# Start addresses on chip: normed activations on a 64-byte multiple, the arena 32 bytes above one

## The reference

```
h = rms_norm(x);  proj = h @ w_in                 # 1024 x 7168
m = rms_norm(mem);  mk, mv = split(m @ w_mem_kv)  # 1024 x 1024
merged = sum_b sigmoid(gate_b) * (attention_b(proj, mk, mv) @ w_branch_b)   # three kinds of attention
x = x + merged @ w_out
x = x + moe(rms_norm(x))     # 32 experts, top 4: (up + 1) * gate * sigmoid(1.702 gate), then w_down
out = rms_norm(x)
```

## Time and profile before

| | |
|---|---|
| median of 3 executions | 1217.89 us (1217.21 to 1218.4) |
| the profiled execution | 1218.3 us, its span 1216.5 us |
| granted TensorE clock, mean | 0.984 |
| TensorE matmul busy | 1166.8 us |
| moved by DMA | 455.15 MB, mean 374 GB/s |

### The profile page before, as it was taken

One profiled execution on the slowest core, in us unless ns is written; L12 is line 12 of the kernel. 1 busy time (PEld: TensorE's weight loads), 2 busy tenths in 40 slices (PEclk: granted clock), 3 DMA queues, 4 the chain that ended last, 5 costly groups with the idle time before them and its releaser, 6 DMA issues.

```text
span 1216.5 us, 14185 instructions
## 1 busy us (share of the span) xinstructions
PE 1166.8 (96%) x6145; PEld 595.8 (49%) x6145; DVE 246.4 (20%) x511; ACT 269.7 (22%) x579; POOL 206.4 (17%) x89
## 2 busy tenths in 40 slices
PE   8999999999999999999999999998999999999996
PEld 7989877898433333333343333333333333333332
DVE  3145132233411121111111211111111111111112
ACT  6457577445210111001010100100000000010002
POOL 5864766785000000000000000000000000000000
PEclk9999999999999999999999999999999999999999
DMA  8775644677999999999999999999999999999994
GB/s 278 262 244 198 212 155 154 226 278 256 424 430 431 430 434 434 415 435 432 431 432 432 430 434 433 433 432 433 433 430 431 431 430 432 430 432 431 431 431 207
DMA packets 62136, 455.15 MB, mean 374 GB/s; under 512 B 5129, under 2 KB 33705, under 8 KB 43512
## 3 DMA queue, kind: packets, MB, share of 16 engines
q1 hardware_dynamic: 62072, 454.22, 90.3%
HBM read 453.13 MB, written 1.07 MB: 373 GB/s over the span
## 4 chain that ended last, share of the span: by engine, by line
PE 65%; DMA 30%; ACT 2%; DVE 1%; POOL 1%; issue 1%; DVEq 0%; SPq 0%; ACTq 0%; POOLq 0%
PE ps L591 63%; DMA arena<-in_expert_w_gate_up 27%; DMA arena<-in_expert_w_down 3%; PE ps L904 1%; PE ps L646 1%; PE ps L898 1%; POOL w_lowc L580 0%; DMA arena<-in_mem 0%; POOL w_lowa L580 0%; ACT arena L1106 0%; ACT arena L1096 0%; ACT L1120 0%; ACT w_high L1076 0%; DVE x_normed L1562 0%; PE ps L642 0%
## 5 line engine op out<-in xcount | busy, mean ns | idle before, releaser
L591 PE MATMUL ps<-arena,gathered_T 128*64 128x512 f32 x2034 | 472.8, 613 | 29.2 <-DMA arena<-in_expert_w_gate_up 29.2
L591 PE MATMUL ps<-arena 128*64 128x512 f32 (+6 forms) x1490 | 316.4, 562 | 3.4 <-issue 2.1
L591 PEld LDWEIGHTS ps<-arena,gathered_T 128*64 128x64 f32 x2034 | 144.9, 140 | 296.5 <-issue 269.2
L591 PEld LDWEIGHTS ps<-arena 128*64 128x64 f32 (+3 forms) x1490 | 113.3, 149 | 196.2 <-issue 193.6
L1229 ACT COPY arena<-ps 128x256 f32<-128x256 f32 x32 | 11.9, 372 | 350.5 <-PE ps L898 350.5
L1506 DVE TENSOR_SCALAR arena<-arena 128x128 f32<-128x128 f32 x64 | 19.3, 344 | 307.2 <-PE ps L898 307.2
L1512 DVE TENSOR_SCALAR arena<-ps 128x512 f32<-128x512 f32 x32 | 22.1, 692 | 275.6 <-PE ps L591 275.6
L1220 ACT ACTIVATE gathered_T<-ps,g_cols 128x128 f32<-128x128 f32 x128 | 36.6, 368 | 173.4 <-PE ps L591 173.4
L591 PEld LDWEIGHTS ps<-arena,x_normed 128*128 128x128 f32 x512 | 59.5, 191 | 24.8 <-issue 24.3
L591 PE MATMUL ps<-arena,x_normed 128*128 128x128 f32 x512 | 65.4, 281 | 0.2 <-DVE arena L1463 0.2
L1239 ACT COPY arena<-ps 128x512 f32<-128x512 f32 x31 | 18.2, 586 | 172.2 <-PE ps L591 172.2
(11 more groups left out here) (229 smaller groups left out, 897.5 us busy)
## 6 DMA issues: line engine op xcount, KB each, us to landing
arena<-in_expert_w_gate_up SPq DMA_DIRECT2D x53, 4096.0 KB, 37.9
arena<-in_expert_w_down SPq DMA_DIRECT2D x61, 2048.0 KB, 38.2
arena<-in_expert_w_gate_up SPq DMA_DIRECT2D x19, 2048.0 KB, 10.8
arena<-in_w_in SPq DMA_DIRECT2D x29, 1024.0 KB, 5.2
arena<-in_expert_w_down SPq DMA_DIRECT2D x6, 1024.0 KB, 38.6
arena<-in_expert_w_gate_up SPq DMA_DIRECT2D x4, 1024.0 KB, 7.1
arena<-in_w_out SPq DMA_DIRECT2D x4, 1024.0 KB, 5.8
arena<-in_w_mem_kv SPq DMA_DIRECT2D x3, 1024.0 KB, 11.5
```

The source lines that it names most:

```text
L591: return nc.tensor.matmul(out, lhsT, rhs, start=start, stop=stop, **kw)
```

## The change

`eps` is allocated behind `h_T_parts`, no longer ahead of `x_tokens`. So `x_tokens` starts at 3328, `x_normed` at 11520, `h_T_parts` (with all that lies over it) at 19712: multiples of 64. What follows `eps` stands where it stood. The arena's start is rounded up to 64 and then raised by 32: it starts at 38944, 32 above a multiple of 64, and everything in it moves by 32. No instruction, DMA, wait or size changes.

```
-        eps = sb("eps", [P, 1])
         x = sb("x_tokens", [P, T, D])
         xn = sb("x_normed", [P, T, D])
         hHL = sb("h_T_parts", [P, 2, KC, S], F32R)
         h_at = nc.sbuf_base - 2 * KC * S * 4
+        assert h_at % 64 == 0
+        eps = sb("eps", [P, 1])
...
-        base = -(-nc.sbuf_base // 64) * 64
+        base = -(-nc.sbuf_base // 64) * 64 + 32
         MOE0 = RING * CHUNK
         arena = nc.alloc_sbuf_tensor_at("arena", [P, ARENA], F32, offset=base)
```

## The result

The changed kernel is slower: 1223.78 us median (1222.56 to 1225.81, 6 runs) against 1217.55 us (1215.71 to 1218.4, 6 runs) of the kernel before beside it, a ratio of 1.0054 [1.0043, 1.0065]. That is outside the range. All lines of the code stand one number higher in the changed kernel.

A forecast was written before the change was run, and what follows sets the result against it. PE bounds the front, transfers the expert stage from 307 us. Front matmul terms +0.9 - 0.5 - 1.6 + 0 gave -1.2 us, passed whole to the end: 1216.7 us against 1217.89, range 1213.4 to 1219.6.

The forecast's parts named there:

- Transfers into the arena: Expert weights landing 32 bytes higher: no loss taken; other end 1.4% of 881 us, 12 us.
- the fourth rival: Expert stage: transfers pay for the new start, visible from 3.6 us, at 1.4% about 1229 us; chance 0.05.
- Group 1: Front, twelve chunks with activations moving, 576 matmuls of 256 columns: 118.3 ns each, +0.9 us.
- group 2: Front, seven single chunks, 336 matmuls with activations stationary: 116.7 ns each, -0.5 us.
- group 4: Front, operand pairs within the arena (memory, branches, output): both operands move alike, 0 us.
- Group 3: Front, ten wide chunks, 240 matmuls of 512 columns, activations stationary: 226.7 ns each instead of 233.3, -1.6 us.
- only the difference counts: Front matmuls: only the two operand addresses' difference matters, so a swap does nothing, 1217.9 us; chance 0.17.
- the matmuls of the experts: Expert stage, float32 matmuls on PE: no loss, and any would be hidden under the transfers; nothing taken.
- ACT's casts: ACT's 82 casts: 1047 ns at remainder 0, 1046 at 32; nothing taken, bounds 0.1 us.
- falling GB/s: Full stretches of the expert stage should stay at 431 GB/s; a fall would make the prediction wrong.
- the price of a stationary operand: Rival for front matmuls: stationary operand 32 above a multiple costs 6.7 ns anywhere, +3.1 us, 1221.0 us; chance 0.07.

The follow-up runs named there:

- small loads and 32: Arena 32 bytes higher, against the small loads kernel with the arena at 38912: 1241.18 us, ratio 1.0201.
- relation kept: Kernel before with normed parts 32 below a multiple of 256, arena on one (39168), so arena minus normed parts as in the changed kernel: 1218.23 us, ratio 1.0005.
- small loads: Kernel before with weights of experts 4 to 30 (without 6 and part of 8) loaded chunk by chunk in 8 KB packets: 1225.41 us, ratio 1.0062.

## Why the prediction was wrong

**The step that failed** is "*Transfers into the arena.* ... I take nothing". It measured 4.1 us in the stream of expert weights, the fourth rival come true at a price between its 3.6 us of visibility and its 12: I gave it 0.05 and left it out of the range. Two things went wrong in that step. The one is the remainder: I had sorted every row by the remainder by 64, by which the arena at 38912 and one at 39040 are alike, while the runs tell the transfers apart by 256. The other is the witness. x's load to a start 32 above a multiple went at 444 GB/s, and I called that too rough for 0.2%. It was worse than rough: in the trace of before x's own packets of 8 KB take 309 ns at that very start, no price at all, and in the kernel with only the arena moved the same load to the same address takes 314 (medians). In all four kernels with x there and the arena off the boundary (32, 64, 128, small loads and 32) its median packet takes 313 or 314 ns, in the four with x there and the arena on it (before, 256, relation kept, small loads) 309. A single load off a boundary among others on it was no witness for a stream off it.

The Trainium skill had spoken against the change: DMA: Bandwidth & Descriptors, section "How a descriptor splits into AXI transactions", names the 256-byte boundary and a price per descriptor. It tells of bytes that are fetched, while what moved here is where the rows are written. The runs agree on both, the boundary (0 and 256 free, 32, 64 and 128 paid) and the price per row and not per byte. Its size does not agree: by that rule 32 bytes off costs one beat of 32 bytes, an estimate of 1.2 ns at the 16384 bytes in 611 ns of a row, and 128 bytes off four beats, 4.8 ns. Measured are 4.1 ns and, for 128, 2.9. I set that rule aside on the strength of a row that could not decide.

**Pairs of the front.** Group 1 held (+1.5 x 576 = +0.9 us), group 2 held (-0.5), group 4 held at nothing (memory pairs 119.8 and 119.6 ns, branches 228.1 in both). Between the first wide memory run and the bias load behind PE's last front chunk lie 297.41 - 26.14 = 271.27 us and before 297.68 - 26.83 = 270.85: +0.4, their sum. That this load was issued 0.3 us earlier, and not later, comes from a start 0.7 us earlier, which differs from execution to execution.

**Group 3** was mis-sized: -1.6 us forecast, 0 measured. I let the stationary operand's place decide. The table says that the difference of the two addresses does: before and with everything 256 higher, the same three durations; the changed kernel, the arena 64 higher and the kept relation, with three different pairs of places, again one set. Each difference tried but 0 (32, 96 and 224) leaves the wide products near 233; 0 gives 228. So the rival "only the difference counts" was right on what counts and wrong on what follows: the difference changes its sign, from 32 below to 32 above, and the two groups of 256 columns trade durations.

**The rest** held: the DMA share stays full, the matmuls of the experts and ACT's casts don't change, and PE in the expert stage stays covered by the transfers. What I said would make the prediction wrong, falling GB/s, is what did. Two small sums were off, without consequence: by its own words the range ends at 1217.9 + 1.9 = 1219.8 us, not 1219.6, and the price of a stationary operand decides from 5.3 ns on, not 5.4.

**What stays open.** The kernels with the arena off a multiple lose some 6 us by the medians, the packets from 330 us on account for 4.1. Of the profiles, the five off a multiple issue the bias load at 299.0 us on average (297.4 to 300.8), the five on one at 297.2 (296.0 to 298.4). The front, where 8 and 16 KB rows pay from 30 to 140 us and the 1 and 2 KB rows ahead of 30 us, seems to end 1 to 2 us later, of which the matmuls explain at most 1.1; single executions scatter too much to say where.

## What to carry to other kernels

Before a buffer that takes a stream of transfers is moved, take its start by 256 and not by a smaller number that suits the engines, and count the rows that go into it: in the saturated stream here each cost its few nanoseconds, 0.5% with rows of 16 and 32 KB and 1.3% with rows of 8 KB. If two operands have to stand apart for PE, move the small one, as the kept relation did, and leave the stream's buffer on its boundary. A sum of nanoseconds on an engine is not the sum of the change as long as the resource that ends last, here the transfers, has only a rough window as its witness: the duration of single packets is the row to look for.

## What the runs showed that was not expected

- The price does not grow with the distance from the boundary: 4.1 ns for 32 bytes, 3.2 for 64, 2.9 for 128 (16 KB rows). Part of the fall is that fewer packets pay: at 128 bytes 22% of them took at most the 611 ns of before, at 64 bytes 6%, at 32 almost none. Those above 611 ns took, without the slowest tenth, 615.0, 614.4 and 615.0 ns at 32, 64 and 128.
- It is not always paid. In the changed kernel the 16 KB packets of 210 to 240 us took 611 ns into the same arena, those from 30 to 120 us 616 to 618, and from 330 us on nearly all pay. Rows of 1 KB between 8 and 14 us took 48 to 51 ns in the five kernels off a multiple and 46 in the others, those of 2 KB between 14 and 30 us 88 and 84; from 30 to 330 us all ten kernels have 46 and 84 (medians). In the kernel before, x's load 32 above a multiple did not pay. What turns it on isn't known; nothing here was run for it.
- Float32r matmuls of 256 columns came out at 116.7 to 119.9 ns and those of 512 at 228.4 to 233.9. In the ten kernels they go by the difference of their operands' addresses, and its remainder by 128 doesn't sort them: differences of 96 and 224, alike by 128, give 119.9 and 118.3 ns for the single chunks. The remainder by 256 does.
- Loads of 8 KB rows cost less than their packets say: 7.7 us more than before, where the packet durations gave 12 to 13. Why is open.
